# Expert weight loads as 16 KB runs per partition, with the contraction index of the expert products permuted to match

## What is computed

```python
def _hier_moe(x, w_coarse, b_coarse, w_fine, b_fine, w_gate, w_up, w_down):
    ...                                     # routing: one group of 4, then 2 of its 8 experts
    gate = jnp.zeros((n, N_EXPERTS), f32).at[jnp.arange(n)[:, None], eidx].add(wt)
    hg = jnp.einsum('nd,edf->nef', xs, w_gate)
    hu = jnp.einsum('nd,edf->nef', xs, w_up)
    act = jax.nn.silu(hg) * hu * gate.astype(x.dtype)[:, :, None]
    out = jnp.einsum('nef,efd->nd', act, w_down)
```

## Time and profile before

| | |
|---|---|
| time, median of 3 runs | 1865.99 us (1861.5 to 1869.1) |
| profiled execution, first to last instruction | 1859.5 us |
| TensorE busy with matmuls | 1491.5 us, 80% of the span |
| VectorE, GpSimd, ScalarE busy | 32%, 16%, 15% |
| moved by DMA | 505.25 MB, mean 272 GB/s |
| mean granted TensorE clock | 0.902 of full speed |

### The profile page before, as it was taken

How to read it: one execution, slowest core, us unless ns; L and a number is a source line. 1 busy time by engine, 2 the same in 40 slices (tenths; PEclk the granted TensorE clock), 3 DMA queues, 4 the chain that set the end, 5 groups by cost and what they waited for, 6 DMA issues and landing times.

```text
span 1859.5 us, 19166 instructions
## 1 busy us (share of the span) xinstructions
PE 1491.5 (80%) x7437; PEld 845.5 (45%) x7437; DVE 589.6 (32%) x1466; ACT 274.7 (15%) x501; POOL 292.6 (16%) x402
## 2 busy tenths in 40 slices
PE   6898898879989996887777777878777788787780
PEld 5676666667757774432333333323333333333230
DVE  2789999856653223100100101001001001010015
ACT  2100001233330000110111111111111111111011
POOL 0055555433300000000000000000000000000006
PEclk9999899999998997998989999988988887899895
DMA  9333222433516444899999999999999999999964
GB/s 286 110 110 117 91 91 91 127 114 118 162 36 198 145 177 161 328 393 399 377 393 368 363 396 378 383 383 379 373 376 371 383 383 376 389 383 388 362 261 149
DMA packets 253053, 505.25 MB, mean 272 GB/s; under 512 B 23572, under 2 KB 99556, under 8 KB 233708
## 3 DMA queue, kind: packets, MB, share of 16 engines
q1 hardware_dynamic: 235788, 493.74, 73.7%
q0 software_dynamic: 5200, 9.19, 1.6%
q10 hardware_dynamic: 12016, 1.66, 0.6%
HBM read 503.18 MB, written 26.28 MB: 285 GB/s over the span
## 4 chain that ended last, share of the span: by engine, by line
DMA 35%; PE 25%; SPq 6%; DVE 1%; POOL 1%; issue 1%; ACT 0%; POOLq 0%; ACTq 0%; DVEq 0%
DMA ring<-in_w_up_dram 34%; PE bank L1254 16%; PE bank L1184 6%; SPq L378 6%; PE bank L1275 1%; PE bank L893 1%; DMA ring<-expert_rows 0%; PE bank L1151 0%; PE bank L1134 0%; POOL arena L855 0%; POOL arena L856 0%; PE bank L1162 0%; DVE arena L1791 0%; PE bank L1204 0%; PE bank L1221 0%
## 5 line engine op out<-in xcount | busy, mean ns | idle before, releaser
L1254 PE MATMUL bank<-ring,arena 128*64 128x512 f32 x2048 | 512.1, 656 | 149.1 <-DMA ring<-in_w_up_dram 149.1
L1254 PEld LDWEIGHTS bank<-ring,arena 128*64 128x64 f32 x2048 | 199.6, 150 | 434.6 <-issue 434.6
L1275 PE MATMUL bank<-ring,arena 128*64 128x512 f32 x1024 | 270.3, 689 | 19.0 <-DVE arena L1778 19.0
L1773 DVE SCALAR_TENSOR_TENSOR arena<-arena,gcol 64x512 f32<-64x512 f32 x32 | 23.8, 744 | 712.8 <-ACT arena L718 712.8
L923 PE MATMUL bank<-arena,ring 128*128 128x280 f32 x768 | 193.8, 413 | 4.0 <-ACT arena L573 2.6
L923 PEld LDWEIGHTS bank<-arena,ring 128*128 128x128 f32 x768 | 149.0, 196 | 47.5 <-issue 8.6
L1275 PEld LDWEIGHTS bank<-ring,arena 128*64 128x64 f32 x1024 | 83.2, 156 | 182.6 <-issue 182.6
L832 POOL DMA_INDIRECT expert_rows<-arena,idx_dst x32 | 29.5, 921 | 799.6 <-ACT arena L723 799.6
L723 ACT ACTIVATE arena<-bank 64x512 f32<-64x512 f32 x128 | 75.9, 593 | 342.5 <-PE bank L1275 341.4
L1184 PE MATMUL bank<-ring,arena 128*128 128x256 f32 x512 | 115.5, 387 | 0.0
L1221 PE MATMUL bank<-ident,arena 64*128 64x64 f32 x721 | 67.2, 242 | 57.6 <-DVE arena L1773 44.8
(11 more groups left out here) (333 smaller groups left out, 1406.9 us busy)
## 6 DMA issues: line engine op xcount, KB each, us to landing
ring<-in_w_down_dram SPq DMA_DIRECT2D x64, 2048.0 KB, 21.0
ring<-in_w_gate_dram SPq DMA_DIRECT2D x64, 2048.0 KB, 19.5
ring<-in_w_up_dram SPq DMA_DIRECT2D x64, 2048.0 KB, 22.6
ring<-in_w_in_dram SPq DMA_DIRECT2D x20, 2048.0 KB, 8.3
ring<-in_w_out_dram SPq DMA_DIRECT2D x8, 2048.0 KB, 9.5
ring<-in_s_w_glu_dram SPq DMA_DIRECT2D x2, 2048.0 KB, 8.3
arena<-v_samples SPq DMA_DIRECT2D x8, 512.0 KB, 4.3
ring<-expert_rows SPq DMA_DIRECT2D x4, 1024.0 KB, 9.1
```

Source lines behind the costliest of these rows:

```text
L1254: ins = pe.matmul(PB[b][at:at + CAP, :], xgT[b][:, kk, :], slot(s, KD // 2)[:, k, :], start=(kk == 0), stop=(kk == KD - 1))
L1275: ins = pe.matmul(PB[2 + cc // 2][at:at + CAP, :], hT[:, f, :], slot(4 + half, KF // 2)[:, k, cc * 512:(cc + 1) * 512], start=(f == 0), st ...
```

## The change

The rows of a half are dealt out to the partitions differently: partition p of a half now holds the consecutive rows 8p to 8p + 7 (gate and up) or 2p and 2p + 1 (down), which is one piece of 16 KB in memory. Step k of a product then contracts over the rows 8p + k, so that its other operand must have the same order: the transposes take every eighth column of the gathered rows, and every second column of the hidden activations, within the same half. The gain must stand in that order too: a new tile `ffn_gain` is loaded with one more DMA on SP, at the start of the program behind the other small vectors, and VectorE waits once for it ahead of the expert loop and reads it in place of `vecs`. The matmuls, their number, their shapes and the bytes moved stay as they are.

```diff
 def load_gate_up(e, q):
...
-                sp.dma_start(slot(MOE_SLOT[q], KD // 2), src.rearrange("a (k p) n -> p (a k) n", p=P)) \
+                sp.dma_start(slot(MOE_SLOT[q], KD // 2), src.rearrange("a (p k) n -> p (a k) n", p=P)) \
                     .then_inc(slot_loaded[MOE_SLOT[q]], 16)
 def load_down(e, s):
...
-                sp.dma_start(slot(s, KF // 2), src.rearrange("a (k p) n -> p (a k) n", p=P)) \
+                sp.dma_start(slot(s, KF // 2), src.rearrange("a (p k) n -> p (a k) n", p=P)) \
                     .then_inc(slot_loaded[s], 16)
 def load_vectors():
...
+                sp.dma_start(ffn_gain[:, :, :], t["norm_ffn"][0].rearrange("(h p k) -> p h k", h=2, p=P)).then_inc(gain_loaded, 16)
 def transpose_rows(p):
                 for k in range(KD):
-                    ins = turn_64(PB[4 + k // 8][:, (k % 8) * CAP:(k % 8 + 1) * CAP], xg[p][0:CAP, k * P:(k + 1) * P], k == 0)
+                    half, kk = divmod(k, KD // 2)
+                    rows = xg[p][0:CAP, half * (D // 2):(half + 1) * (D // 2)].rearrange("t (p k) -> t k p", k=KD // 2)[:, kk, :]
+                    ins = turn_64(PB[4 + half][:, kk * CAP:(kk + 1) * CAP], rows, k == 0)
                 ins.then_inc(tr_done, 1)
 def round_pe(R):
...
                         for f in range(KF):
-                            ins = turn_64(PB[6][:, f * CAP:(f + 1) * CAP], hh[0:CAP, f * P:(f + 1) * P], f == 0)
+                            half, kf = divmod(f, KF // 2)
+                            cols = hh[0:CAP, half * (FH // 2):(half + 1) * (FH // 2)].rearrange("t (p k) -> t k p", k=KF // 2)[:, kf, :]
+                            ins = turn_64(PB[6][:, f * CAP:(f + 1) * CAP], cols, f == 0)
 # VectorE, ahead of the expert loop, and in rows_in
             nc.vector.engine_nop().then_inc(h_made, 1)
+            dve.wait_ge(gain_loaded, 16)
             dve.wait_ge(lists_ready, 1)
...
-                              vecs[:, V_FFN + 8 * q:V_FFN + 8 * q + 8].unsqueeze(2).broadcast_to([P, 8, CAP]), ALU.mult)
+                              ffn_gain[:, q, :].unsqueeze(2).broadcast_to([P, 8, CAP]), ALU.mult)
```

More of the change, by code:

```diff
@@ L108, in hymba_step @@
         vecs = sb("vecs", [P, 80])
+        ffn_gain = sb("ffn_gain", [P, 2, KD // 2])
         sc5 = sb("sc5", [P, 6, NJ])
@@ L261, in hymba_step @@
         x_loaded = [sem(f"x_loaded{i}") for i in range(3)]
-        vec_loaded, s5_loaded, bc_loaded, wr_loaded = sems("vec_loaded s5_loaded bc_loaded wr_loaded")
+        vec_loaded, s5_loaded, bc_loaded, wr_loaded, gain_loaded = sems("vec_loaded s5_loaded bc_loaded wr_loaded gain_loaded")
         slot_loaded = [sem(f"slot_loaded{i}") for i in range(6)]
```

## The result

The changed kernel takes 1850.55 us (median of 10 runs, 1840.35 to 1858.28), the kernel before 1862.53 us (10 runs). The ratio is 0.9925, with an interval from 0.9907 to 0.9942: faster by 0.75%, or 12 us. The forecast was 1794 us and its range ended at 1847 us, so the change brought a sixth of what was expected. The profiled execution has a span of 1849.7 us, and the mean granted clock is 0.877 where it was 0.902.

The account below looks back on a forecast made before the run. The DMA rate of the weight loads was taken as the bound: 74.9 us saved by longer runs, less 2.5 us for the small rest, takes 72.4 us off 1865.99 us, giving 1794 us; range 1772 to 1847 us.

Parts of the forecast that it names:

- the line: Weight loads: time per packet, drawn through 2 KB (387 GB/s) and 8 KB (425 GB/s); 16 KB gives 432 GB/s, saving 74.9 us.
- the price at 425 GB/s: Weight loads: the lower bound if nothing is won beyond 8 KB packets, 60.1 us saved in all.
- The rival by which the run length doesn't count: Weight loads: 425 GB/s has another cause, loads stay at 34.0 us an expert, 1868 us; chance 0.07.
- the transposes: TensorE's strided row transposes: a halved read costs 0.9 us an expert, covered by its wait for weights.
- The rival with dear strides: Strided transposes costing over 2.6 us more an expert make the kernel slower, 1886 to 1994 us; chance 0.10.
- the small rest: Start and ends: the new DMA, transposes that nothing hides and VectorE's new wait cost 2.5 us in all.
- the loop of the gathers: Down product, copies, scatter, gather, transposes: 32.3 us an expert, with 1.0 us more each for gather and scatter.
- the step that chose the bound: Expert loop: with 32.3 us for the gather loop against 31.6 us for the loads, the loads were taken as bound.
- The rival at the middle of the loop: Gather loop last at 32.3 us in place of 34.0 an expert: saves 51 us less 2.5, giving 1817 us.
- the gather loop becomes last: Rival: the gather loop bounds the experts, 1817 us at 32.3 us or 1847 us at 33.3 us an expert; chance 0.22.
- its refutation: Signs named as proving it wrong: loads stay at 387 GB/s, late gathers awaited in most experts, or 17 transposes taking 4 us.

Follow-up runs that it names:

- the other order: The kernel before, with GpSimd issuing the gather for expert x + 2 ahead of the scatter of expert x: 1855.4 us, ratio 0.9952.
- the 12 matmuls: The changed kernel plus 12 unread 128x512 matmuls between the gate and up matmuls and the wait for the gather: 1854.95 us, ratio 0.9963.
- the kernel with small loads: The changed kernel with all experts but the first loading a quarter of their weights, output wrong, other work the same: 1649.47 us.
- the fastest version: The changed kernel (16 KB runs) with GpSimd's gather issued ahead of the scatter: 1797.82 us, ratio 0.9649; in a second set 1795.85 us, ratio 0.9629.
- the kernel with 24: The changed kernel plus 24 unread 128x512 matmuls, all on one half of a bank, ahead of the wait for the gather: 2264.39 us.

## Why the prediction was wrong

**Right: what bounded the kernel before, and what the loads can do.** The loads were last there: only 8 us come from the other order. With the gather out of the way the cycle is 31.48 us, forecast 31.6 us. Stages full of 16 KB packets move 424 to 437 GB/s, where the line gave 432; but over the whole kernel the gain is at the low end, 57.6 us, just the price at 425 GB/s (60.1 less 2.5). The rival by which the run length doesn't count falls with this: the same matrices in longer runs are 57.6 us faster once the gather is out of the way.

**Right: the transposes.** 0.9 us an expert was forecast, 1.1 us measured, and the loads covered it (ratio 0.9996). At full clock 17 of them take 2.33 us, as forecast, where they took 1.36 us. The rival with dear strides had needed 4.0 us. Those of the activations, put at nothing, cost 0.16 us (0.78 us, where they took 0.62). Both in an expert of the kernel with 16 KB and the gather first, at a granted clock of 1.00:

```profile
1196.87 2.33 PE L1231 MATMUL bank<-ident,arena 64*128 64x64 f32 x17
1200.46 0.78 PE L1231 MATMUL bank<-ident,arena 64*128 64x64 f32 x5 [1.26 <-DVE arena L1789]
```

**Not to be told: the small rest.** 2.5 us were forecast for the start and the ends. The first copy of the up part starts 2.7 us later than before (761.4 us against 758.7). But it starts anywhere from 757.7 to 761.8 us in the kernels with the new DMA, and at 759.9 us in the other one without it.

**Nearly right: the loop of the gathers.** The prediction sized it at 32.3 us, with its middle for the down product. The same parts, from the end of one down product to the end of the next, as means over 29 experts of the trace after (the fourth to the last; without the last one, whose gather lands in 2 us, the sum is 33.4 us):

| part | forecast | after |
|---|---|---|
| end of down product to scatter | 3.23 | 3.27 |
| scatter to gather | 7.56 + 1.0 | 7.82 |
| gather to transposes | 7.52 + 1.0 | 9.07 |
| transposes and VectorE's copy | 3.11 + 0.9 | 3.73 |
| down product | 7.94 | 9.29 |
| sum | 32.26 | 33.18 |

Scatter and gather together cost 16.9 us where 17.1 was forecast; that is partly luck, for the scatter was put 0.7 us too high and the gather 0.55 us too low. The term that was mis-sized is the down product, by 1.35 us. I had taken the middle between 7.09 us and 8.78 us. Already before, the mean over all 32 was 8.45 us (from 7.09 to 10.1), which is 0.5 us of it. After, it is 9.28 us, and all but the last take 8.46 us or more. These 0.8 us go with the new place of the wait. In the 30 experts between the first and the last TensorE stands idle for 5.1 to 7.4 us ahead of the transposes, and every one of their down products starts at the granted clock of 0.50; the mean clock over the down products is 0.76, and was 0.85 before. In all kernels here whose transposes wait for the gather in most experts the mean is 9.2 or 9.3 us; where the gather is issued first it is 8.3 to 8.5 us. That the clock would come back without the idle time was not shown: the 12 matmuls shortened it and changed nothing.

**Wrong: the step that chose the bound.** "But if the loop is last, the loads' queue runs dry for a moment in each expert, and in a quiet queue a landing takes 3.2 us: the loop then shortens itself. I take the loads as the bound." The sum had 32.3 us for the loop and 31.6 us for the loads, so the loop was the longer by my own numbers, and this sentence alone turned the choice. Its first half is right, the queue runs dry. The short landing is right for the scatter (3.2 us in the kernel with small loads) and half right for the gather (4.6 us). What is wrong is that both meet. The dry moment comes 6 to 9 us ahead of the scatter, in the down product, and by the time of the scatter TensorE has released the down slots, behind them the gate and up slots. So the landings stayed at 6.6 us and 9.0 us, and the loop did not shorten. The gap and the landings hang on the same event, TensorE's progress, and keep their distance (5.6 to 5.8 us in every expert with a gap). This was to be seen before: the order of SP's loads and the places of scatter and gather in the earlier trace rows give it.

This step alone does not make the number. The rival at the middle of the loop, 32.3 us, stood at 1817 us, 23 us above the forecast. Of the other 33 us the longer loop explains (33.18 - 32.26) x 30 = 28 us, and that is the down product.

**The rival that came true** is "the gather loop becomes last", and its mechanism was right. Its price was right by luck: 33.3 us an expert and 1847 us stood there, 33.23 us and 1850.55 us were measured, but that price was for 1.5 us more each in gather and scatter. The time went into the down product, and gather and scatter together took less than with 1.0 us each. The rival's chance of 0.22 rested on the step that failed. The observation that the prediction named as its refutation, gathers that land later than 9 us and a line of transposes that waits for them in most experts, is nearly what the trace shows (a median of 9.0 us; L1223 waits 31 times).

## What to carry to other kernels

When two loops are within a few per cent, the longer one by the sum is the bound, unless a row shows the mechanism that shortens it at the very place where it waits. A faster bulk transfer gives its gain only down to the next loop; a small transfer that has to go through the same engines is worth moving off the chain first (here GpSimd's order: 8 us by itself, 53 us on top of the long runs). For a duration that takes two values, take the mean over all of its instances and not the middle; and where a wait moves to another place, ask which work will stand behind it, for here that work became slower by 0.8 us.

## What the runs showed of the hardware

- The cost of a strided stationary read differed with the clock. At 1.00 the 17 and 5 transposes take 2.33 + 0.78 us, where the plain ones took 1.37 + 0.62 us. At 0.50 the 22 take 3.14 us (the row 1328.20:1331.40 of the changed kernel), and the plain ones behind the same wait 3.03 us. At the lower level the stride cost 0.1 us of 3 us here. A stage of the fastest version, with 22 strided transposes at full clock (2 of its 24 are the last gate and up matmuls):

```profile
1226.75:1229.90 3.15, 3.12 (x24) 2.84 (x22) 0.81 (x2) 1.28 (x2) 0.00 (x0) 1.00 1.00 427
```

- In the kernel with 12 more matmuls the clock was 1.00 up to the transposes and fell to a mean of 0.63 while they ran, although TensorE was busy for 3.15 of the 3.20 us; 1.7 us of idle time lay before them. In the kernel with 24 the transposes did not wait and ran at 1.00, TensorE stood still for 0.6 us, and the clock still fell in the down product behind them in about every second expert:

```profile
1700.00:1703.20 3.20, 2.61 (x23) 2.48 (x23) 0.56 (x2) 0.00 (x0) 0.00 (x0) 1.00 0.00 0
1703.20:1707.00 3.80, 3.80 (x10) 1.22 (x12) 1.33 (x3) 0.00 (x0) 0.00 (x0) 0.56 0.00 0
```

- Beside loads in 16 KB packets the gather lands 1.6 us later than beside those of before (9.0 and 7.4 us), and the scatter no later (6.6 and 6.8 us). Why was not settled.
